# A long transformer kernel on one core: the gate and up projection as seven block products in place of eight

## The reference

```python
def swiglu(h, w_gate_up, w_down):       # h 512 x 1024, w_gate_up 1024 x 5632, w_down 2816 x 1024
    gu = jnp.einsum("bsd,df->bsf", h, w_gate_up)
    g, u = jnp.split(gu, 2, axis=-1)
    return jnp.einsum("bsf,fd->bsd", jax.nn.silu(g) * u, w_down)
```

## Time and profile before

| what | value |
|---|---|
| time, median of 3 runs | 1367.54 us (1366.03 to 1367.59) |
| time of the profiled execution | 1366.49 us |
| its span, first to last instruction | 1364.8 us |
| mean granted TensorE clock | 0.995 |
| PE busy | 99% of the span |
| DVE, ACT, POOL busy | 49%, 43%, 18% |

### The profile page before, as it was taken

One profiled execution on the slowest core, in us unless ns is written; L12 is line 12 of the kernel. 1 busy time (PEld: TensorE's weight loads), 2 busy tenths in 40 slices (PEclk: granted clock), 3 DMA queues, 4 the chain that ended last, 5 costly groups with the idle time before them and its releaser, 6 DMA issues.

```text
span 1364.8 us, 16782 instructions
## 1 busy us (share of the span) xinstructions
PE 1347.4 (99%) x6486; PEld 1076.6 (79%) x6486; DVE 662.9 (49%) x1493; ACT 583.7 (43%) x1322; POOL 240.0 (18%) x207
## 2 busy tenths in 40 slices
PE   8999999999999999999999999999999999999999
PEld 7777778888889888888888787877777777777687
DVE  4415555333552433334223746566666656666632
ACT  4325455322443332323113436455655565556620
POOL 3012220000031000000000422241423224243300
PEclk8999999999999999999999999999999999999999
DMA  6312222223362423332134321222223222222331
GB/s 236 101 40 61 70 70 62 93 93 95 109 228 63 138 83 119 92 93 93 63 125 173 132 93 62 72 84 85 70 72 99 71 70 70 72 87 82 124 124 62
DMA packets 110096, 130.76 MB, mean 96 GB/s; under 512 B 7488, under 2 KB 87360, under 8 KB 110016
## 3 DMA queue, kind: packets, MB, share of 16 engines
q1 hardware_dynamic: 104400, 112.39, 26.0%
q10 hardware_dynamic: 5616, 17.30, 3.4%
HBM read 120.24 MB, written 9.44 MB: 95 GB/s over the span
## 4 chain that ended last, share of the span: by engine, by line
PE 90%; DVE 5%; ACT 3%; issue 1%; POOL 1%; DMA 0%; ACTq 0%; POOLq 0%; DVEq 0%
PE ps L710 14%; PE ps L712 14%; PE ps L711 14%; PE ps L715 12%; PE ps L717 12%; PE ps L716 12%; PE ps L930 3%; DVE wlo L1250 2%; PE ps L940 1%; PE ps L915 1%; ACT px L1201 1%; PE ps L964 1%; PE ps L742 1%; PE ps L814 1%; PE ps L955 1%
## 5 line engine op out<-in xcount | busy, mean ns | idle before, releaser
L1250 DVE TENSOR_TENSOR wlo<-raw,whi 128x512 fp32r<-128x512 f32 x308 | 215.1, 729 | 300.6 <-ACT whi L993 300.2
L993 ACT ACTIVATE whi<-raw 128x512 fp32r<-128x512 f32 (+1 forms) x388 | 224.3, 612 | 213.6 <-PE ps L712 103.0
L710 PE MATMUL ps<-whi,hth 128*128 128x512 f32 x592 | 248.9, 420 | 1.3 <-DVE wlo L1250 1.3
L715 PE MATMUL ps<-hth,whi 128*128 128x512 f32 (+1 forms) x608 | 239.5, 394 | 0.0
L717 PE MATMUL ps<-hth,wlo 128*128 128x512 f32 (+1 forms) x608 | 234.3, 385 | 0.0
L716 PE MATMUL ps<-htl,whi 128*128 128x512 f32 (+1 forms) x608 | 234.1, 385 | 0.0
L712 PE MATMUL ps<-wlo,hth 128*128 128x512 f32 x592 | 232.7, 393 | 0.0
L711 PE MATMUL ps<-whi,htl 128*128 128x512 f32 x592 | 231.8, 392 | 0.0
L1585 POOL TENSOR_TENSOR wlo<-raw,whi 128x512 fp32r<-128x512 f32 (+1 forms) x80 | 96.6, 1222 | 655.3 <-ACT whi L993 655.3
L710 PEld LDWEIGHTS ps<-whi,hth 128*128 128x128 f32 x592 | 111.5, 188 | 33.5 <-issue 9.5
L715 PEld LDWEIGHTS ps<-hth,whi 128*128 128x128 f32 x608 | 114.6, 188 | 26.8 <-issue 4.9
(11 more groups left out here) (305 smaller groups left out, 1987.2 us busy)
## 6 DMA issues: line engine op xcount, KB each, us to landing
raw<-in_l_w_in SPq DMA_DIRECT2D x64, 512.0 KB, 4.8
raw<-in_w_gate_up SPq DMA_DIRECT2D x44, 512.0 KB, 5.0
raw<-in_w_in SPq DMA_DIRECT2D x14, 1024.0 KB, 5.3
raw<-in_w_down SPq DMA_DIRECT2D x10, 1024.0 KB, 5.1
raw<-in_l_w_out SPq DMA_DIRECT2D x8, 1024.0 KB, 5.2
raw<-in_w_in SPq DMA_DIRECT2D x24, 256.0 KB, 3.7
raw<-in_w_branch SPq DMA_DIRECT2D x8, 512.0 KB, 4.1
raw<-in_w_out SPq DMA_DIRECT2D x4, 1024.0 KB, 5.1
```

The costliest lines, as they stand in the source:

```text
L710: e.matmul(o, ah, wh[:, cs], start=a, stop=False)
L715: e.matmul(o, wh[:, cs], ah, start=a, stop=False)
L993: return e.activation(out, in_, ACT.Copy, **how)
L1250: return e.tensor_tensor(out, src, hi_part.bitcast(F32), ALU.subtract)
```

## The change

Groups 1 to 10 of `gate_up` are each taken as a product of 2 x 2 blocks. A is the input: A11 and A12 the first 256 tokens by the first and second half of the width, A21 and A22 the other 256 tokens. B is the group's weights: B11 and B21 the gate columns (first and second half of the width), B12 and B22 the up columns. In place of eight products of such blocks there are seven, each of 24 matrix instructions of 128x256 (2 outputs of 128 columns x 4 tiles x 3): 168 for a group, 1680 for the ten. For them sums are wanted. Of the input, once: POOL adds high and low parts of A11 and A12 back together, DVE forms four sums of 128 x 1024 (`sl_f`), ACT and DVE split them (`sh`, `sl`); that is the step `hs`. Of the weights, in each group: POOL makes four sums of 128 x 1024 into `ts`, each from the one before or from `raw` (step `wt`). ACT and DVE split the seven blocks, three plain and four sums, whole (128 x 1024) into four quarters of `whi`/`wlo`, so that block b waits for product b - 4 (step `ws`). The seven results are combined by DVE with five additions or subtractions that read PSUM, by ACT with one copy and two Silus, and DVE multiplies twice from SBUF (step `gx`); the product gate times up is kept as plain fp32 in `gu`, which lies where `gul` lies. `sh`, `sl_f` and `ts` lie where `guh` lies, so the splitting of `gu` into `guh` and `gul` comes at the end of `gate_up` and during the down projection (step `gs`, eleven of 128 x 1024), and `dn_k` of the first column half begins with tiles 16 to 19. Group 0 is computed as before. Arithmetic is the same up to rounding.

```diff
+BLOCKS = ["B11", "T3", "B21", "T2", "T1", "T4", "B22"]
+BANKS = [0, 1, 0, 2, 3, 4, 3]
+SUMS = ["T3", "T2", "T1", "T4"]
+RING = [2, 3, 6, 7, 0, 1, 4, 5]
+LASTJ = 10
...
-        self.dn_k = [[0, 4, 8, 12, 16, 20], [20, 0, 4, 8, 12, 16]]
+        self.dn_k = [[16, 0, 4, 8, 12, 20], [20, 0, 4, 8, 12, 16]]
...
+        self.h[self.mix].pre = []
...
+        put("hs")
+        for i in range(3):
+            put("wt", 1, i)
+        put("ws", 1, 0)
+        put("ws", 1, 1)
...
+                if c == 0 and i < 5:
+                    k1 = W.dn_k[0][i + 1]
+                    for k in range(k1, min(k1 + 4, KF), 2):
+                        put("gs", k)
...
-        for j in range(11):
-            n = self.W.mix + 2 * j
-            if j == 0:
-                order = [(p, a, t) for p in range(2) for t in range(4) for a in range(2)]
-            else:
-                order = [(None, a, t) for a in range(2) for t in range(4)]
-            for p, a, t in order:
-                yield from self.unit(n + a, 16 if p is None else 32, 4, "gu", j, p, a, t)
-                if a == 1 and p != 0:
-                    self.put("guo", j, t)
-                yield
+        for p, a, t in [(p, a, t) for p in range(2) for t in range(4) for a in range(2)]:
+            yield from self.unit(self.W.mix + a, 32, 4, "gu", p, a, t)
+            if a == 1 and p == 1:
+                self.put("guo", t)
+            yield
+        self.put("ws", 1, 2)
+        self.put("ws", 1, 3)
+        self.put("wt", 1, 3)
+        for j in range(1, LASTJ + 1):
+            for p in range(7):
+                for q in range(4):
+                    self.put("gp", j, p, q)
+                    yield
+                self.put("gx", j, p)
+                if p < 3:
+                    self.put("ws", j, p + 4)
+                elif j < LASTJ:
+                    self.put("wt", j + 1, p - 3)
+                    self.put("ws", j + 1, p - 3)
+                elif p == 3:
+                    self.owners[-1] = ("gp", j, 4, 3)
+                    self.owners.append(("gp", j, 6, 3))
+                elif p == 4:
+                    self.put("gs", 16)
+                    self.split(self.W.dn, 1)
+                elif p == 5:
+                    self.put("gs", 18)
+                    self.split(self.W.dn, 3)
+                else:
+                    self.split(self.W.dn, 4)
...
+                elif kind == "gp":
+                    j, p, q = a
+                    b, fb = BANK(j, p), q // 2
+                    if q == 0:
+                        if p == 2:
+                            pe.wait_ge(snap_a, j)
+                        elif p == 6:
+                            pe.wait_ge(comb_d, COMB(j, C22))
+                        else:
+                            claim(b)
+                        pe.wait_ge(blk_lo, BLOCK(j, p) + 1)
+                        if S_LO[p]:
+                            pe.wait_ge(s_lo, S_LO[p])
+                    wh, wl = slot_of(j, p)
+                    o = ps[b][:, 256 * fb:256 * fb + 256]
+                    for kt in (2 * (q % 2), 2 * (q % 2) + 1):
+                        cs = slice(256 * kt + P * fb, 256 * kt + P * fb + P)
+                        ah, al = moving[p](kt)
+                        z = kt == 3
+                        e.matmul(o, wh[:, cs], ah, start=q == 0 and kt == 0 and p not in (2, 6), stop=False,
+                                 skip_group_check=True)
+                        e.matmul(o, wh[:, cs], al, start=False, stop=False, skip_group_check=True)
+                        m = e.matmul(o, wl[:, cs], ah, start=False, stop=z, skip_group_check=True)
+                    m.then_inc(mm, 1)
...
+                        pe.wait_ge(gu_lo, GU(min(k0 + 2, KF - 1)))
...
+                elif kind == "ws":
+                    j, p = a
+                    if BLOCKS[p][0] == "B":
+                        n = W.mix + 2 * j + int(BLOCKS[p][1]) - 1
+                        act.wait_ge(raw_in[n % 3], H[n].landed)
                     else:
-                        act.wait_ge(gm_d, 2 * j + i + 1)
-                        copy(guh[:, 2 * j + i, :], tf[i][:, 512:1024]).then_inc(gu_hi, 1)
+                        act.wait_ge(t_p, 4 * (j - 1) + SUMS.index(BLOCKS[p]) + 1)
+                    b = BLOCK(j, p)
+                    if b >= 4:
+                        act.wait_ge(mm, PRODUCT(1 + (b - 4) // 7, (b - 4) % 7))
+                    else:
+                        act.wait_ge(mm, H[W.mix - 2 if b < 2 else W.mix + 1].done)
+                    copy(four(slot_of(j, p)[0]), block_of(j, p)).then_inc(blk_hi, 1)
+                elif kind == "gx":
+                    j, p = a
+                    o = ps[BANK(j, p)][:, :]
+                    if p == 0:
+                        act.wait_ge(mm, PRODUCT(j, 0))
+                        if j > 1:
+                            act.wait_ge(comb_d, COMB(j - 1, U2))
+                        else:
+                            act.wait_ge(gm_d, 2)
+                        copy(p1_t, o).then_inc(snap_a, 1)
+                    elif p == 2:
+                        act.wait_ge(mm, PRODUCT(j, 2))
+                        if j > 1:
+                            act.wait_ge(comb_d, COMB(j - 1, GU0))
+                        e.activation(sg0_t, o, ACT.Silu).then_inc(sg0_a, 1)
+                    elif p == 5:
+                        act.wait_ge(comb_d, COMB(j, C21))
+                        e.activation(c21_t, c21_t, ACT.Silu).then_inc(sg1_a, 1)
+                elif kind == "gs":
+                    k, = a
+                    if k >= 16:
+                        act.wait_ge(blk_lo, BLOCK(LASTJ, 5) + 1)
+                    else:
+                        act.wait_ge(mm, PRODUCT(LASTJ, 6))
+                    if k >= 2:
+                        act.wait_ge(comb_d, COMB(k // 2, GU0))
+                    copy(guh[:, k:k + 2, :], gu[:, k:k + 2, :]).then_inc(gu_hi, 1)
...
+                elif kind == "hs":
+                    dve.wait_ge(af_p, 1)
+                    for t in range(2):
+                        a21 = ps[PJ[2 + t]][:, :].rearrange("p (k t) -> p k t", k=4)
+                        tok = slice(P * t, P * t + P)
+                        dve.wait_ge(ht_pe, HT(1, 2 + t))
+                        e.tensor_tensor(sl_f[2][:, :, tok], sl_f[0][:, :, tok], a21, ALU.subtract).then_inc(s_d, 1)
+                    for t in range(2):
+                        a22 = ps[HI4[2 + t]][:, :].rearrange("p (k t) -> p k t", k=4)
+                        tok = slice(P * t, P * t + P)
+                        dve.wait_ge(s_d, t + 1)
+                        e.tensor_tensor(sl_f[1][:, :, tok], a22, sl_f[2][:, :, tok], ALU.subtract).then_inc(s_d, 1)
+                    dve.wait_ge(s_d, 4)
+                    e.tensor_tensor(sl_f[0][:, :, :], sl_f[1][:, :, :], sl_f[0][:, :, :], ALU.add).then_inc(s_d, 1)
+                    dve.wait_ge(af_p, 2)
+                    e.tensor_tensor(sl_f[3][:, :, :], sl_f[3][:, :, :], sl_f[1][:, :, :], ALU.subtract).then_inc(s_d, 1)
+                    for i, to in enumerate((2, 1, 0, 3)):
+                        dve.wait_ge(s_hi, i + 1)
+                        dve.wait_ge(s_d, 6)
+                        lower(sl[to][:, :, :], sl_f[to][:, :, :], sh[to][:, :, :]).then_inc(s_lo, 1)
+                elif kind == "ws":
+                    j, p = a
+                    wh, wl = slot_of(j, p)
+                    dve.wait_ge(blk_hi, BLOCK(j, p) + 1)
+                    lower(four(wl), block_of(j, p), four(wh)).then_inc(blk_lo, 1)
+                elif kind == "gx":
+                    j, p = a
+                    o = ps[BANK(j, p)][:, :]
+                    if p == 3:
+                        dve.wait_ge(snap_a, j)
+                        dve.wait_ge(mm, PRODUCT(j, 3))
+                        e.tensor_tensor(u2_t, o, p1_t, ALU.add).then_inc(comb_d, 1)
+                        dve.wait_ge(comb_d, COMB(j, U2))
+                        e.tensor_tensor(u3_t, ps[BANK(j, 1)][:, :], u2_t, ALU.add).then_inc(comb_d, 1)
+                    elif p == 4:
+                        dve.wait_ge(comb_d, COMB(j, U3))
+                        dve.wait_ge(mm, PRODUCT(j, 4))
+                        e.tensor_tensor(c22_t, o, u3_t, ALU.add).then_inc(comb_d, 1)
+                    elif p == 5:
+                        dve.wait_ge(mm, PRODUCT(j, 5))
+                        e.tensor_tensor(c21_t, u3_t, o, ALU.subtract).then_inc(comb_d, 1)
+                    elif p == 6:
+                        dve.wait_ge(sg1_a, j)
+                        dve.wait_ge(comb_d, COMB(j, C22))
+                        e.tensor_tensor(gu[:, 2 * j:2 * j + 2, 256:512], pair(c21_t), pair(c22_t),
+                                        ALU.mult).then_inc(comb_d, 1)
+                        dve.wait_ge(mm, PRODUCT(j, 6))
+                        e.tensor_tensor(u2_t, o, u2_t, ALU.add).then_inc(comb_d, 1)
+                        dve.wait_ge(comb_d, COMB(j, C12))
+                        dve.wait_ge(sg0_a, j)
```

(29 more changed lines are left out.)

125 lines of the change are left out of this document (89 added, 36 removed).

## The result

The changed kernel took a median of **1355.28 us** (4 runs, 1354.06 to 1356.68), the kernel before beside it 1366.91 (4 runs, 1366.03 to 1367.59): ratio 0.9916, 95% interval 0.9898 to 0.9933, so 11.6 us faster. On another chip it was 1355.62. The profiled execution took 1356.68 with a span of 1354.9, 9.9 less than the span before.

A forecast was written before the change was run, and what follows sets the result against it. PE's stream of matrix instructions was taken to bound the kernel. The terms, -217.6 + 201.6 + 9.7 + 2.0 + 2.6 = -1.7 us, gave 1366 us, own range 1361 to 1369, or 1358 to 1378 with most of two rivals.

The forecast's parts named there:

- the start: Before group 1's first product: PE waits 9.7 us for `wlo0<-raw2`, behind turns of POOL and DVE.
- Products on PE: Groups 1 to 10: 1680 instructions of 128x256 at 0.120 take 201.6 us, replacing 217.6.
- Rival 4: Groups 1 to 10: PE at 0.1135 all through; DVE and POOL then set the pace, 1364; chance 0.08.
- The clock: Behind the wait before group 1's first product: PE's clock falls to half, costing 2.0 us.
- The end: At the down projection's first rows: PE waits 0.9 and 1.7 us, together 2.6 us.
- A steady group: Each block group: PE sets the pace at 20.16 us, with 1.6 us of POOL's work needing to overlap DVE's PSUM rows or gaps.
- rival 2: Block groups: DVE and POOL set the pace, 20.7 to 21.8 us a group, 1372 to 1382; chance 0.30.
- The turns: DVE rows with both inputs in SBUF and POOL's exclude one another; DVE's 1024 rows take up to 3.6 us.
- Rival 3: Before group 1's first product: shorter wait, 2.8 to 5 us, clock hardly falls, 1357 to 1361; chance 0.20.

The follow-up runs named there:

- e1: Changed kernel with six 128x512 subtractions added on POOL ahead of the first block group's two input additions: 1362.03 us.
- e7: Kernel before, with gate and up products of ten groups issued as 1920 instructions of 256 columns in place of 960 of 512: 1378.73 us.
- e8: Changed kernel with one 128x512 subtraction added on POOL in each block group, ahead of the third weight sum: 1361.21 us.
- e2: Changed kernel with POOL's weight sums cut to 8 columns of each tile, products reading an unsummed block instead: 1352.28 us.
- e13: Changed kernel with two 128x512 POOL subtractions per group behind the fourth sum, and one lower part moved behind DVE's addition after product 5: 1355.11 us.
- e3: Changed kernel with one of POOL's four weight sums in each block group done twice: 1365.46 us.
- e5: Changed kernel with splits reordered around the end of the block groups, down-projection pieces split behind products five and six: 1352.49 us.
- e11: Changed kernel with one lower part of the next group's first block moved behind DVE's addition after product 5, no added POOL work: 1355.58 us.
- e4: Changed kernel with the first product's block split ahead of the input sums: 1354.67 us.

## Why the prediction was wrong

**The step that failed** is in the part on the start: "DVE's first new row waits for POOL's first addition, and POOL is busy with two pieces until 415.86." Those pieces are the split of the half that follows the mixed one (`mix+2`). The diff takes it away (`self.h[self.mix].pre = []`), and I had taken the pieces for the half before it. So POOL's first addition starts 7.75 us sooner, at 408.11, and the wait is 1.95 us in place of 9.7. That 9.7 - 7.75 gives just this number is luck, as the chain after it changed too. By starts the wait is 7.5 shorter, in three parts. DVE's first new row no longer waits for POOL's first addition; it follows its own `htl` rows at 414.36 and not at 418.3 (3.9). From there to the first product it is 14.8 us and not 17.5 (2.7), since POOL's third sum is over before the lower parts begin. And PE itself comes 0.9 later.

e1 puts work back in front of POOL's additions and most of the wait with it, 7.88 us. There the chain as predicted is seen, 17.1 us for 17.5. So the mechanism behind the step, turns of POOL and DVE on the way to `wlo0<-raw2`, was right; with a wait of 2 us the sum would have been near 1358.

**Products on PE**: 201.6 forecast; 199.7 measured (201.2 less the low clock's 1.5). The four products with `sh` and `sl` go at 0.118, the three with `hth` and `htl` at 0.120, so 19.97 a group and not 20.16. I had read from the earlier trace rows that the weights decide; here these are `whi` and `wlo` in all seven, and the time goes with the other operand. e7 shows 0.120 as the price of the shape. Rival 4 (0.1135 all through) is out. The closest in any run are single products behind a wait: 24 starts in e8, from 488.91 on, are 0.1133 apart. No product of the ten groups in any run goes at the 109 ns of the Trainium skill (TensorE: Matmul & The Clock Gate, Back-to-back issue gap). The page gives it for a matmul by itself and says that at small widths it leaves out the weight loads of a real stream.

**The start**: 9.7 forecast, 1.95 measured (2.1 by starts). **The clock**: 2.0 forecast, 1.5 measured in this execution; it isn't in every one (last section). **The end**: 2.6 forecast, 2.2 by the recorded waits, 2.5 by starts; both at the places named. Together -217.6 + 199.7 + 2.1 + 1.5 + 2.5 = -11.8, against -1.7.

**A steady group**: the outcome (PE sets the pace, no waits) was right, as e2 shows. The budget beside it was not. I had 1.6 us of room in a sum of two engines' work. The runs show 0.82 at one place, found by what waits there, and beyond that, as far as the rows tell, DVE's queue: 2.4 to 2.5 us of additional POOL work cost 0 (e13) to 1.2 us a group (e3), by where it stands. So rival 2 was nearer than its 1.6 said: 1.3 us of work on POOL was enough for it.

**The turns** of POOL and DVE are confirmed: POOL's sums take 2.41 alone and 3.2 to 3.4 beside DVE; DVE's 1024 rows 1.22 and up to 3.42; `xf<-ps,tf` 0.67 to 0.69 in every run. This is the rule of the Trainium skill (SBUF — State Buffer, Who interferes with whom) that I weighed: an instruction of DVE with two inputs in SBUF contends with one of POOL that reads SBUF, one with a single SBUF input doesn't (the page excepts modes that no run here shows). In this kernel it costs nothing in the groups, since DVE has some 3.5 us of gaps in each (about 0.5, 1.4 and 1.65).

Rival 3 named the right side, at 1357 to 1361 (measured 1355.3), but for another reason: the exclusion was in full force (2.91 and 3.42), POOL was only further on when DVE came.

## What to carry to other kernels

Before a wait is worked out from "engine X is busy until", say which step of the program that work is, and look whether the change removes it: a one-line edit of a list can delete the row on which the chain starts. Room in a loop of several engines is first of all the distance at each hand-over between the producer's end and the consumer's start, not the sum of the work: with one lower part in the wrong place, small additions elsewhere cost 5 to 6.5 us, nearly all of which a change of order gave back. When an algorithm saves multiplications but halves the columns of each instruction, charge the shape first: here it took a third of the saving.

## What was unexpected of the hardware

The clock fell to half for 3.4 us behind a wait of just 1.95 us in the changed kernel, and again behind 1.96 on another chip; behind 7.88 us in e1 it was low for as long, from 433.81 to 437.20. Yet the same wait was followed by no step of 0.213 in the first product of e5 (1.91), e11 (1.95) and e13 (1.90). In e11:

```profile
429.22 0.36 PE L998 MATMUL ps<-hth,whi 128*128 128x256 f32 x1 [1.95 <-DVE wlo L1411]
...
429.89 0.28 PE L1001 MATMUL ps<-hth,wlo 128*128 128x256 f32 x1
430.01 0.28 PE L998 MATMUL ps<-hth,whi 128*128 128x256 f32 x1
```

So at this length the wait alone does not tell whether the clock falls, and the 1.5 us are a cost of some executions; what decides stays open. Behind the waits of 0.57 and 1.16 us in e4 no step of 0.213 follows.

Second, 256-column instructions run at 0.118 with `sh` and `sl` and at 0.120 with `hth` and `htl` as the operand beside the same weights; the operands' layouts differ (256 columns in a row against half of 512). That can't be all of it, since in the earlier trace rows the same `hth` goes at 0.1175 beside `yah` and at 0.120 beside `whi`. No run takes this apart, so the cause stays open.
